# Group norm of the SSD branch: the sum of squares split into two rounded parts and spread over all partitions first, root and reciprocal taken on the spread rows

## What is computed

```
def grouped_rmsnorm(y, g, n_groups):
    shp = y.shape
    yf = y.astype(jnp.float32).reshape(*shp[:-1], n_groups, shp[-1] // n_groups)
    yf = yf * lax.rsqrt(jnp.mean(yf * yf, axis=-1, keepdims=True) + EPS)
    return yf.reshape(shp) * g
...
    y = y.reshape(bsz, seqlen, SSD_D_INNER) * jax.nn.silu(z.astype(jnp.float32))
    return grouped_rmsnorm(y, norm_g, SSD_N_GROUPS).astype(z.dtype)
...
    y_ssd = ssd_branch(z, xbc, dt_raw, ...) @ w_ssd_out
```

## Time and profile before

| | |
|---|---|
| time, median of 3 runs | 1481.81 us (1481.76 to 1481.86) |
| span of the profiled execution | 1480.0 us |
| that execution around its span | no device time of its own is shown; the median is 1.81 us above the span |
| busy: PE, PEld | 1470.0 us (99%), 1209.8 us (82%) |
| busy: DVE, ACT, POOL | 815.5 us (55%), 523.2 us (35%), 960.9 us (65%) |
| mean granted TensorE clock | 0.999 |

### The profile page before, as it was taken

How to read it: one execution, slowest core, us unless ns; L and a number is a source line. 1 busy time by engine, 2 the same in 40 slices (tenths; PEclk the granted TensorE clock), 3 DMA queues, 4 the chain that set the end, 5 groups by cost and what they waited for, 6 DMA issues and landing times.

```text
span 1480.0 us, 22968 instructions
## 1 busy us (share of the span) xinstructions
PE 1470.0 (99%) x8098; PEld 1209.8 (82%) x8098; DVE 815.5 (55%) x1132; ACT 523.2 (35%) x935; POOL 960.9 (65%) x945
## 2 busy tenths in 40 slices
PE   8999999999999999999999999999999999999999
PEld 7788887888788888888988888888888888888887
DVE  3567696577578647322655545500267483746723
ACT  4481651362262121112622222200242554636441
POOL 5456667676766789898167777799426554655544
PEclk9999999999999999999999999999999999999999
DMA  9244434533633344635022333334223222222231
GB/s 378 88 136 137 134 101 133 166 113 120 192 99 113 117 138 157 140 116 198 16 91 93 99 99 99 100 127 143 72 96 122 75 84 72 71 72 70 73 127 72
DMA packets 67982, 172.04 MB, mean 116 GB/s; under 512 B 7728, under 2 KB 24496, under 8 KB 66512
## 3 DMA queue, kind: packets, MB, share of 16 engines
q1 hardware_dynamic: 45504, 150.05, 30.8%
q10 hardware_dynamic: 22416, 21.18, 4.6%
HBM read 166.94 MB, written 4.27 MB: 116 GB/s over the span
## 4 chain that ended last, share of the span: by engine, by line
PE 98%; DVE 1%; ACT 1%; DMA 0%; issue 0%; SPq 0%; DVEq 0%; ACTq 0%
PE ps L620 17%; PE ps L623 17%; PE ps L622 17%; PE ps L637 6%; PE ps L639 5%; PE ps L638 5%; PE ps L991 4%; PE ps L990 4%; PE ps L989 4%; PE ps L891 1%; PE ps L1181 1%; PE ps L1256 1%; PE ps L1257 1%; PE ps L1258 1%; PE ps L1016 1%; PE ps L1012 1%
## 5 line engine op out<-in xcount | busy, mean ns | idle before, releaser
L570 POOL TENSOR_SCALAR w_hi<-raw 128x512 fp32r<-128x512 f32 x386 | 256.6, 683 | 488.1 <-PE ps L623 228.5
L575 POOL TENSOR_TENSOR w_lo<-raw,w_hi 128x512 fp32r<-128x512 f32 x386 | 540.7, 1422 | 0.0
L620 PE MATMUL ps<-h_hi,w_hi 128*128 128x512 f32 x880 | 347.4, 395 | 0.2
L623 PE MATMUL ps<-h_hi,w_lo 128*128 128x512 f32 x880 | 342.8, 390 | 0.0
L622 PE MATMUL ps<-h_lo,w_hi 128*128 128x512 f32 x880 | 342.5, 389 | 0.0
L620 PEld LDWEIGHTS ps<-h_hi,w_hi 128*128 128x128 f32 x880 | 165.2, 188 | 38.1 <-issue 5.0
L623 PEld LDWEIGHTS ps<-h_hi,w_lo 128*128 128x128 f32 x880 | 165.2, 188 | 35.1
L622 PEld LDWEIGHTS ps<-h_lo,w_hi 128*128 128x128 f32 x880 | 165.3, 188 | 34.5 <-issue 1.0
L637 PE MATMUL ps<-h_hi,w_hi 128*128 128x512 f32 x352 | 140.7, 400 | 0.0
L639 PE MATMUL ps<-h_hi,w_lo 128*128 128x512 f32 x352 | 137.4, 390 | 0.0
L638 PE MATMUL ps<-h_lo,w_hi 128*128 128x512 f32 x352 | 137.1, 390 | 0.0
(11 more groups left out here) (442 smaller groups left out, 2855.9 us busy)
## 6 DMA issues: line engine op xcount, KB each, us to landing
raw<-stream SPq DMA_DIRECT2D x231, 512.0 KB, 3.3
ada_raw<-ada SPq DMA_DIRECT2D x64, 256.0 KB, 3.6
ada<-ada_first SPq DMA_DIRECT2D x8, 1024.0 KB, 14.8
abc<-acs_dram ACTq DMA_DIRECT2D x16, 512.0 KB, 7.0
raw<-stream SPq DMA_DIRECT2D x8, 256.0 KB, 12.1
xr<-x_classes ACTq DMA_DIRECT2D x1, 2048.0 KB, 10.1
x_dram<-xr ACTq DMA_DIRECT2D x1, 2048.0 KB, 7.8
x_res<-x_dram ACTq DMA_DIRECT2D x2, 1024.0 KB, 9.2
```

Source lines behind the costliest of these rows:

```text
L570: nc.gpsimd.tensor_scalar(hi[:, w], raw[:, raw_slot, w], 1.0, 1.0, ALU.mult, ALU.mult).then_inc(split_hi, 1)
L575: ins = nc.gpsimd.tensor_tensor(lo[:, w], raw[:, raw_slot, w], hi[:, w].bitcast(F32), ALU.subtract)
L620: nc.tensor.matmul(ps[:, bank], hi[:, w], x_hi[:, k0 + k], start=start and k == 0, stop=False)
L623: mm = nc.tensor.matmul(ps[:, bank], lo[:, w], x_hi[:, k0 + k], start=False, stop=stop and k == tiles - 1)
```

## The change

`column_sums` and `spread_roots` are replaced by `group_sums`, one place earlier: after `conv(0)` in the loop, before unit 1 of the mix. The sum of squares `sct` is rounded by ScalarE into `xst_hi`, VectorE takes the rest into `xst_lo`, and TensorE multiplies both with a matrix of ones in fp32r. So the sum over the partitions stands on all partitions at once. ScalarE takes the root of that 128 x 512 bank into `sct`, VectorE writes the reciprocal of the 128 x 512 tile into bank 4, and `scale_y` reads it as before.

```diff
+            def group_sums(g):
+
+                pe.wait_ge(gate_steps, 1 + 16 * g + 7)
+                pe.wait_ge(y_squared, 1 + 2 * g + 2)
+                pe.wait_ge(setup, 8)
+                nc.tensor.matmul(ps[:, 4], ones_r[:], xst_hi[:], start=True, stop=False)
+                nc.tensor.matmul(ps[:, 4], ones_r[:], xst_lo[:], start=False, stop=True).then_inc(group_sum, 1)
...
                     conv(0)
+                    group_sums(g - 1)
                     conv(1)
-                    column_sums(g - 1)
                     conv(2)
-                    spread_roots(g - 1)
                     conv(3)
...
-                if i == 2:
-                    column_sums(GROUPS - 1)
-                if i == 3:
-                    spread_roots(GROUPS - 1)
+                if i == 1:
+                    group_sums(GROUPS - 1)
...
+                def square_hi():
+                    act.wait_ge(gate_steps, 1 + 16 * g + 6)
+                    A(xst_hi[:], sct[:], ACT.Copy).then_inc(y_squared, 1)
...
             def roots(g):
-                act.wait_ge(group_sum, 2 * g + 1)
-                A(small[:, 8:12], ps[:, 4, 0:4], ACT.Sqrt, bias=eps[:, 0:1], scale=1.0 / S).then_inc(group_root, 1)
+                act.wait_ge(group_sum, 1 + g + 1)
+                A(sct[:], ps[:, 4], ACT.Sqrt, bias=eps[:, 0:1], scale=1.0 / S).then_inc(group_root, 1)
...
             def invert_roots(g):
                 dve.wait_ge(group_root, 1 + g + 1)
-                V.reciprocal(small[:, 12:16], small[:, 8:12]).then_inc(gate_steps, 1)
-                dve.wait_ge(gate_steps, 1 + 16 * g + 7)
-                TT(sct[:].rearrange("p (c t) -> p c t", c=NT), ident.unsqueeze(1).broadcast_to([P, NT, P]),
-                   small[:, 12:16].unsqueeze(2).broadcast_to([P, NT, P]), ALU.mult).then_inc(gate_steps, 1)
+                V.reciprocal(ps[:, 4], sct[:]).then_inc(gate_steps, 1)

             def scale_y(g):
-                dve.wait_ge(group_sum, 2 * g + 2)
+                dve.wait_ge(gate_steps, 1 + 16 * g + 8)
...
+                def square_lo():
+                    dve.wait_ge(y_squared, 1 + 2 * g + 2)
+                    TT(xst_lo[:], sct[:], xst_hi[:].bitcast(F32), ALU.subtract).then_inc(gate_steps, 1)
...
                 if first:
                     dt_by_token()
+                    V.tensor_copy(ones_r[:], ones[:]).then_inc(setup, 1)
```

More of the change, by code:

```diff
@@ L195, in build @@
         dec_last = at("dec_last", FREE + 138 * KB + 256, [P, 3, HEADS_G])
+        ones_r = at("ones_r", FREE + 138 * KB + 384, [P, P], F32R)
         xn = at("xn", FREE + 16 * KB, [P, DB, S])
@@ L410, in build @@
         out_stored = sem("out_stored")
-        start_at_one = [group_root, chunk_steps, state_steps, mod_ready, gate_steps, biased,
+        start_at_one = [group_root, group_sum, y_squared, chunk_steps, state_steps, mod_ready, gate_steps, biased,
                         pt_ready, decays, sc_steps, y_done, mix_steps, attended, ada_steps, units_done,
@@ L1474, in group @@
                     square()
+                    square_hi()
                 else:
@@ L2017, in sum_squares @@
                 def sum_squares():
-                    dve.wait_ge(y_squared, g + 1)
+                    dve.wait_ge(y_squared, 1 + 2 * g + 1)
                     V.tensor_reduce(sct[:], xcT[:].rearrange("p b t -> p t b"), AX.X, ALU.add).then_inc(gate_steps, 1)
+                def square_lo():
+                    dve.wait_ge(y_squared, 1 + 2 * g + 2)
+                    TT(xst_lo[:], sct[:], xst_hi[:].bitcast(F32), ALU.subtract).then_inc(gate_steps, 1)
                 def short_conv(q):
@@ L2081, in group @@
                     sum_squares()
+                    square_lo()
                 else:
```

## The result

The changed kernel takes 1491.61 us (median of 5 runs, 1487.02 to 1492.64), the kernel before 1481.76 (1481.24 to 1481.86): a ratio of 1.0061, 95% interval 1.0051 to 1.0072. So it is slower by 0.6%, 9.85 us. The forecast was 1484.3 in a range of 1478.0 to 1488.5: a slower kernel, but only by 2.5 us.

The account below looks back on a forecast made before the run. The prediction took TensorE's own work (98% of the span) as the bound, with VectorE in time by only 0.3 us. -5.5 for matmuls and +8.0 for VectorE's chain gave +2.5 us: 1484.3 us, range 1478.0 to 1488.5.

Parts of the forecast that it names:

- TensorE: removed and added: Column sums and spreading product go (1.83 us a group), two new matmuls come (0.45): 5.5 us less over four groups.
- VectorE: the chain to the last rest: Loop: long reciprocal and turns with GpSimd make the y unit's start 2.65 us late a group, 8.0 us in all.
- The rival of a hidden delay: Loop's VectorE chain: first rest takes an earlier turn, kernel faster by 2.8 to 5.5 us, 1476.9 to 1479.0; chance 0.25.
- that of a turn more: Loop's VectorE chain: third rest misses a turn with GpSimd, TensorE 3.8 + 0.15 us late, 1488.1 us; chance 0.18.
- The early product: Before the new matmuls: their rounded parts are ready at 141.8, wanted at 142.32; at worst 0.6 late once; counted as nothing.
- the second rival: The turn more: third rest starts 0.23 us before GpSimd's first half ends and may miss it; 1488.1 us, chance 0.18.
- The last group: After the loop: `sc_lo` and rests are ready before they are wanted, so the gain of 1.38 us stands.
- the rule in full: VectorE and GpSimd: loser blocked for the other's whole instruction; 4.35 us a group with the restart, 1489.4 us.

Follow-up runs that it names:

- the run without the reciprocal: The run with both edits, its reciprocal replaced by a multiplication by 1.0 into bank 4 (norm not computed): 1476.39 us, ratio 0.9966 to the kernel before.
- the stand-in: The run with both edits, `ada_piece` 2 moved behind the last taps, an equally long instruction with one PSUM input in its place: 1482.43 us, ratio 1.0006.
- the piece ahead of the reciprocal: `ada_piece` 2 moved ahead of the loop's reciprocal: on the run with both edits 1478.57 us (ratio 0.998), on the changed kernel alone 1486.79 us (1.0034).
- the run with both edits: Changed kernel, ones rounded during set-up and the first group's sum of squares rounded by VectorE, not ScalarE: 1487.54 us, ratio 1.0041 to the kernel before.
- the run that kept ScalarE's wait: Changed kernel, first group's sum of squares rounded by VectorE, ScalarE still waiting for that sum: 1492.27 us, ratio 1.006 to the kernel before.

## Why the prediction was wrong

- **TensorE: removed and added** (-5.5): right. The shifts give -5.2, the run without the reciprocal -5.0.
- **VectorE: the chain to the last rest** (2.65 a group): right where the groups run alike. The reciprocal took 3.35 to 3.36, `ada_piece` 2 and the rests the durations that their turns gave, the waits 2.49 (2.64 with the restart). The rival of a hidden delay (its 1476.9 to 1479.0 is 2.8 to 4.9 us under the kernel before, and not up to 5.5) and that of a turn more are both refuted there, and the runs with the stand-in and with the piece ahead of the reciprocal show that it is the turns: with the reciprocal at 3.36 as it was, the wait falls to 0.22.
- The step that failed most is "So 2.65 a group, in the three groups of the loop, which run the same code: 8.0 us". They run the same code, but the first of them starts behind the written-out first group, in which `square_hi` is the last thing that ScalarE does ahead of the loads of `abc`. It measured 5.1, and the sum of the three 10.4 instead of 8.0. From the reciprocal's start to TensorE's it took 20.1 us there and 19.2 in the run with both edits, so of the 2.5 us by which that wait is longer, 1.6 are VectorE's late arrival (1.7 against the forecast's times) and 0.9 are turns: what the second rival described (rests of 3.13 and 3.00) happened here, but from a late start and not by the 0.23 us that it named.
- The reason stands one step earlier, in **The early product**: "I count nothing". There the question was only whether TensorE gets its parts in time, and it does. What is queued behind the rounding on ScalarE, two or three instructions down, was not asked; a wait of 8.54 us had been put in front of three DMA issues. In the same step the rounding of the ones had no price: 1.46 us in the first group, by a turn lost to GpSimd and by what stands behind it.
- **The last group** "has room": `sc_lo` has, as forecast. GpSimd, which takes turns with it, has not: 0.65 us. The sum has +0 there.
- The missing term is the clock. The forecast priced a wait of TensorE at its length and 0.15 for the restart. Behind the first one TensorE ran at half its clock for a while: 2.5 us in the profiled run. The spread of the changed kernel fits that: its run at a mean granted clock of 1.000 took 1487.02, the four at 0.996 to 0.998 took 1490.79 to 1492.64, so 3.8 to 5.6 us more. In the run that kept ScalarE's wait it is the same: one of five took 1486.05 at 0.999, the others 1491.9 to 1492.95 at 0.996 to 0.998. Of the changed kernel's difference 2.5 is located in the profiled run (1491.61, 4.6 more); the other 2.1 can't be, since the run at 1.000 has no profile.

From the forecast's +2.5 to the measured +9.8: +2.4 (first wait), +1.5 (first group), +0.65 (last group), +2.5 (clock), and 0.3 by which the saving was smaller. This is the split of one execution; the forecast's range ended at 1488.5, and one of the five runs of the changed kernel lies within it.

The rule of the Trainium skill that the prediction weighed ("SBUF — State Buffer", "Who interferes with whom") is borne out by the stand-in as to who is blocked: 0.75 us with one SBUF input, 1.50 with two. As to the size, the waits of 2.49 follow the end 0.53 to 0.56 behind GpSimd's that the trace had shown; by the rule in full they would have been 4.2. But the prediction told the rule too widely: "with one SBUF input it never is" holds on that page only outside the two-port modes of VectorE, and here two kinds of instruction with one tile in SBUF as their input, and their output in SBUF, were held: the rounding of the ones, and the pair of line 1891 (2.71 instead of 0.87). So what has to be looked for is not two inputs alone.

Open is why the clock falls behind some waits and not others. In the profiled runs of the six kernels that have a long first wait it fell each time: in all four that waited 4.96 us, and in both that waited 2.48 or 2.49. Of the ten second and third waits of 2.48 or 2.49 us it fell at only two, a second and a third one. It did not fall behind the waits of under 1 us at these places. No run was made that changes only what TensorE does around such a wait.

## What to carry to other kernels

For every instruction that gets a new wait, read its engine's queue behind it until something is found that another engine or a load depends on, DMA issues included. Do it for each copy of the code (the first group, the loop, the last). What stood behind cost more here than the instruction. Where a long instruction lands on a critical chain, move the short ones around it into the wait ahead of it, and not behind it; but first see whose buffers they free, since a load that waits for one holds the whole queue. Where VectorE and GpSimd meet, ask for every instruction whose operands all lie in SBUF which turn it gets: an arrival 1.6 us later cost another 0.9 here. A wait of TensorE costs its length and, at times, its clock.

## What the runs showed of the hardware

- Matmuls of 512 columns stand 0.42 us apart at a granted clock of 0.50 (177.21 to 177.63) and 0.23 at 1.00.
- An instruction of GpSimd can lose to a long one of VectorE what VectorE otherwise loses to it: two instructions of 0.60 each took 3.24 in all beside a rest of 128 x 2048.
- VectorE instructions with one SBUF input lose turns to GpSimd as well: a copy of 128 x 128 with rounding took 1.06 us at 69.44 and ended 0.09 behind GpSimd's instruction, and two of line 1891 took 2.71 instead of 0.87. An instruction of 128 x 512 with one input in SBUF and the other in PSUM lost nothing (0.75).
- TensorE's granted clock fell to 0.50 in or behind all four idle stretches of 4.96 us, in or behind four of the twelve of 2.48 or 2.49, and at none of those under 1 us at these places.
- Three loads of 512 KB issued by ScalarE took 2.93 us at 142.16 and 4.26 at 72.76, with its next instruction behind them, and loads of 256 KB in another queue landed after 8.3 instead of 3.8 us beside them.
